# Second attention done tile by tile in pairs of heads, its output columns behind the heads, tile 1's half of it and of the queries placed among the second layer's gathers

## The chip, the core and the metric

The kernel is one program on one core of a Trainium2 chip. The metric is the time of one execution on the device, in microseconds (us). The core has five engines that each run their own list of instructions in order: TensorE (PE in the profile; its weight loads are PEld), VectorE (DVE), ScalarE (ACT), GpSimd (POOL) and SyncE (SP). They wait for each other through semaphores. Matmul results go to four double banks of PSUM, `psA` to `psD`, of 1024 columns each; everything else lives in SBUF, most of it in one array, `arena`, whose parts are used again by later stages. SyncE starts the plain DMAs, GpSimd the indirect ones (gathers) and a few small ones.

## What is computed

One sequence of 256 tokens, 1024 features, all in float32. The first block (multi-scale pooling and a dilated attention, gated and projected) is not touched here. The second block has two layers. Layer 0 is a short convolution mixer, layer 1 is an attention; each is followed by a mixture of very many small experts, called PEER:

```
x = x + conv_mixer(rmsnorm(x))            # layer 0
x = x + peer(rmsnorm(x), layer 0)
x = x + attention(rmsnorm(x)) @ w_o       # layer 1: 16 heads of 64, 4 key/value heads,
x = x + peer(rmsnorm(x), layer 1)         #   window +-128, bias by distance, a sink logit
return rmsnorm(x)

def peer(t):                               # t: 256 tokens x 1024
    q  = (t @ w_q).reshape(256, 8, 2, 128)          # 8 heads, two half queries each
    sc = q . subkeys                                # 8 x 2 x 128 scores for each token
    16 best of each half, their 256 sums, 16 best of these  -> 16 experts for each head
    g  = softmax(of these 16)
    out = sum over 8 x 16 experts of  g * gelu(t . u[e]) * v[e]
```

`u[e]` and `v[e]` lie side by side in memory, so an expert is one row of 8 KB; 16384 experts in each layer. For each token and each of its 128 choices such a row has to be fetched.

## The kernel before, in words

Tokens are two tiles of 128 (one token in each partition). A PEER layer is 16 units (a head and a tile), tile 0's eight first. A unit is 8 groups of 2 experts. A group goes through a ring of 8 places (4 groups): GpSimd gathers 2 x 1 MB (`gathers`, L478), VectorE takes the dot products with `u` (`dots`, L1364), ScalarE makes gelu, coefficient and a diagonal matrix (`mix`, L604 to L614), TensorE adds diagonal times `v` to the tile's sum in PSUM (`weighted`, L966, four products of 512 columns), and then `ring_free` lets GpSimd gather the group four further on. Between its dots VectorE chooses the next unit's experts (L1300 to L1351).

The queries `t @ w_q` come in four chunks of 512 columns. The first chunk's first head is done tile by tile before the gathers (`first_head`), the others for both tiles at once, in slots behind certain groups (`QUERY_SLOTS`): 8 products of 256 columns (L917) in each slot.

Between the layers stands the second attention. After the last group of layer 0, x is added (L1372), normalised (`norm`: a square on ScalarE, then `Sqrt` there with the load of its table, then a chain on VectorE), transposed (L692), keys and values of tile 1 are made (L702, L997). Then a loop runs over two halves of the heads. Each half computes its queries for both tiles (L1019), spreads them into zeroed buffers (L671), and takes 16 units of one head and one tile in a pipeline: scores (L1029, L1030), bias and maximum (L1443, L1444), exponential (L677), transposes (L1036), copy (L1450), product with the values (L1045), division (L1457). After both halves all is transposed, multiplied with the output weights (`mixer`, L711), added and normalised; then first head, choice of experts, and the second layer's gathers begin. All of it lies between the last group of layer 0 and the first gather of layer 1. The program order written in the code sets the order everywhere; SyncE's order of weight loads (`load`, `load_queries`) with its waits sets when weights arrive.

## Time and profile before

| | us |
|---|---|
| runs shown | 2010.59, 2017.71, 2002.35; median 2010.59 |
| the profiled execution, its own time | 2006.81 |
| span from first to last instruction in it | 2005.0 |
| mean TensorE clock granted | 0.968 of full |
| busy: PE, DVE, ACT, POOL | 1672.7, 1060.0, 573.7, 600.9 |
| moved by DMA | 636.14 MB, of it 541.96 on the software queue |

The profile cuts the span in 40 slices of some 50 us. The share of time in which the DMA engines are busy is 9 tenths or more in the slices of the two gather phases and 3, 2 and 0 tenths between them. In the profile's chain that ended last TensorE has 46% and the gathers 26%. Where a group of rows is called by a line, it is a line of the kernel before; some lines are those of helpers (`norm`, `turn`, `turned_out`, `mixer`) and serve several stages.

### The profile page before, as it was taken

Reading aid. Unit: us, or ns where it says so; the run is one execution under the profiler, and the core shown is the slowest. Engines: PE = TensorE matmul, PEld = TensorE weight load, DVE = VectorE, ACT = ScalarE, POOL = GpSimd, SP = SyncE. Lnnn points to the kernel's source line nnn. Section 1 sums busy time; section 2 is a strip of 40 time slices with the busy share of each in tenths; the row PEclk is TensorE's granted clock in tenths of the full one; section 3 lists DMA queues with packets and bytes.
Section 4 is the critical chain, followed back from the end, with each engine's and each line's share of the span. In section 5 each row is a group of like instructions: output and inputs, shape, how many; then the busy total and the mean of one; then the engine's idle time right before and its main releaser. Section 6 shows DMA issues by size and latency. Waiting matters only on the chain.

```text
span 2005.0 us, 18168 instructions
## 1 busy us (share of the span) xinstructions
PE 1672.7 (83%) x5752; PEld 971.0 (48%) x5752; DVE 1060.0 (53%) x2654; ACT 573.7 (29%) x1679; POOL 600.9 (30%) x533
## 2 busy tenths in 40 slices
PE   7999998997989977778877778979989777777776
PEld 5888885975544522223323257665545322223222
DVE  2113102114576657776677424546666776767664
ACT  2111001002333423334333322223343334333332
POOL 1000000001445444444444300023445444444442
PEclk9999999998999989999999989989999999999999
DMA  8544343447899999999999932089999999999996
GB/s 222 136 136 139 126 152 108 160 157 292 349 421 416 421 417 413 421 391 411 413 421 417 399 130 101 0 308 360 421 413 416 421 421 421 391 421 416 421 421 268
DMA packets 147767, 636.14 MB, mean 317 GB/s; under 512 B 9891, under 2 KB 46771, under 8 KB 81884
## 3 DMA queue, kind: packets, MB, share of 16 engines
q0 software_dynamic: 75152, 541.96, 65.9%
q1 hardware_dynamic: 72524, 93.08, 14.1%
q8 instruction: 43, 0.70, 0.1%
q14 instruction: 48, 0.39, 0.0%
HBM read 633.90 MB, written 1.11 MB: 317 GB/s over the span
## 4 chain that ended last, share of the span: by engine, by line
PE 46%; DMA 27%; DVE 12%; issue 7%; ACT 4%; POOL 4%; DVEq 0%; SPq 0%; POOLq 0%; ACTq 0%
DMA arena<-in_peer_uv,arena 26%; PE ps L966 16%; PE ps L723 9%; DVE arena L1364 5%; PE ps L743 4%; POOL arena L478 4%; PE ps L711 4%; PE ps L702 3%; PE ps L917 3%; PE ps L754 2%; PE ps L1019 1%; ACT arena L614 1%; ACT arena L609 1%; PE ps L692 1%; DVE arena L1303 1%
## 5 line engine op out<-in xcount | busy, mean ns | idle before, releaser
L966 PE MATMUL ps<-arena 128*128 128x512 f32 x2048 | 964.3, 618 | 251.5 <-ACT arena L614 251.2
L478 POOL DMA_INDIRECT arena<-in_peer_uv,arena x512 | 587.8, 1148 | 1176.1 <-PE ps L966 563.2
L1364 DVE CUSTOM_DVE_ANT_0 arena<-xn,arena 128x1024 f32<-128x1024 f32 x512 | 622.1, 1225 | 369.2 <-DMA arena<-in_peer_uv,arena 357.8
L966 PEld LDWEIGHTS ps<-arena 128*128 128x128 f32 x2048 | 384.4, 195 | 809.9 <-ACT arena L614 411.4
L604 ACT ACTIVATE arena<-arena 128x2 f32<-128x2 f32 x256 | 52.0, 203 | 783.5 <-DVE arena L1364 779.3
L614 ACT ACTIVATE arena<-const,arena 128x128 f32<-128x128 f32 x512 | 177.6, 394 | 8.3
L723 PE MATMUL ps<-hT,wbuf 128*128 128x256 f32 x704 | 154.7, 382 | 2.6 <-DVE arena L1241 2.6
L723 PEld LDWEIGHTS ps<-hT,wbuf 128*128 128x128 f32 x704 | 134.6, 192 | 21.6 <-DVE arena L1241 3.0
L609 ACT ACTIVATE arena<-arena 128x1 f32<-128x1 f32 x512 | 123.3, 288 | 8.4
L743 PE MATMUL ps<-hT,wbuf 128*128 128x256 f32 x384 | 86.5, 388 | 2.3 <-DMA wbuf<-in_w_in 2.3
L917 PE MATMUL ps<-hT,wbuf 128*128 128x256 f32 x384 | 86.8, 379 | 0.0
L917 PEld LDWEIGHTS ps<-hT,wbuf 128*128 128x128 f32 x384 | 73.0, 190 | 20.2 <-issue 11.5
L743 PEld LDWEIGHTS ps<-hT,wbuf 128*128 128x128 f32 x384 | 74.4, 195 | 14.0 <-issue 3.5
L702 PE MATMUL ps<-hT,wbuf 128*128 128x128 f32 x576 | 72.7, 290 | 8.6 <-DVE x L1137 2.6
L702 PEld LDWEIGHTS ps<-hT,wbuf 128*128 128x128 f32 x576 | 71.4, 206 | 12.5 <-issue 6.0
L1180 DVE COPY arena<-ps 128x384 f32<-128x384 f32 x16 | 8.6, 555 | 108.4 <-PE ps L780 107.5
L711 PE MATMUL ps<-wbuf,arena 128*128 128x512 f32 x128 | 57.3, 608 | 5.2 <-issue 3.8
L493 ACT ACTIVATE xn<-x 128x1024 f32<-128x1024 f32 x14 | 14.7, 1053 | 117.7 <-DVE x L1137 100.8
L1300 DVE MAX8 arena<-arena 128x8 f32<-128x128 f32 (+1 forms) x96 | 29.0, 330 | 33.5 <-ACT arena L651 21.9
L1249 DVE TENSOR_TENSOR arena<-ps,arena 128x1024 f32<-128x1024 f32 x2 | 2.5, 1225 | 81.4 <-PE ps L723 81.4
...
L604 ACT ACT_TABLE_LOAD x34 | 43.6, 1283 | 0.6
(160 smaller groups left out, 1196.3 us busy)
## 6 DMA issues: line engine op xcount, KB each, us to landing
...
wbuf<-in_peer_w_q SPq DMA_DIRECT2D x8, 2048.0 KB, 8.0
wbuf<-in_w_in SPq DMA_DIRECT2D x7, 2048.0 KB, 8.4
wbuf<-in_conv_w_in SPq DMA_DIRECT2D x6, 2048.0 KB, 10.3
arena<-in_peer_uv,arena POOLq DMA_INDIRECT x512
wbuf<-in_attn_w_qkv SPq DMA_DIRECT2D x3, 2048.0 KB, 20.3
wbuf<-in_w_out SPq DMA_DIRECT2D x2, 2048.0 KB
wbuf<-in_conv_w_out SPq DMA_DIRECT2D x2, 2048.0 KB, 7.9
```

The lines of the kernel that those rows point to most:

```text
L478: pool.indirect_dma_start(ring[:, e % RING], None, A["peer_uv"], bass.IndirectOffsetOnAxis(ap=expert[:, unit % 2, e:e + 1], axis=0))\
L604: nc.scalar.activation(act_e[:, b, e0:e0 + GROUP], dot[:, b, e0:e0 + GROUP], ACT.Gelu).then_inc(gelu_done, 1)
L609: last = nc.scalar.activation(coef[:, b, e:e + 1], act_e[:, b, e:e + 1], ACT.Copy, scale=gate[:, b, e:e + 1])
L614: nc.scalar.activation(diag[:, e % RING], ident, ACT.Copy, scale=coef[:, b, e:e + 1]).then_inc(diag_done, 1)
L702: last = mm(dst[:, m * SEQ + t * P:m * SEQ + (t + 1) * P], wbuf[:, b, k, m * P:(m + 1) * P], hT[:, k, t * P:(t + 1) * P], start=(k == 0), ...
L711: last = mm(ps[j][:, t * 512:(t + 1) * 512], src[:, k, t * P:(t + 1) * P], wbuf[:, b, k], start=(k == 0), stop=(k == KC - 1))
L723: last = mm(dst[:, m * SEQ:(m + 1) * SEQ], wbuf[:, b, k, m * P:(m + 1) * P], src[:, k - k0], start=(k == k0), stop=(k == k1 - 1))
L743: last = mm(dst[:, g * SEQ:(g + 1) * SEQ], wbuf[:, b, k, g * P:(g + 1) * P], hT[:, k], start=(k == 0), stop=(k == KC - 1))
L754: last = mm(psB[:, t * 512 + cols_of.start:t * 512 + cols_of.stop], hT4[:, k, t, first:first + P], wbuf[:, 2, k, cols_of], start=(k == 0), ...
L917: last = mm(psC[:, m * SEQ:(m + 1) * SEQ], wbuf[:, b1, k, m * P:(m + 1) * P], hT[:, k], start=(k == 0), stop=(k == KC - 1))
L966: last = mm(ps[t][:, s * 512:(s + 1) * 512], diag[:, e % RING], ring[:, e % RING, D + s * 512:D + (s + 1) * 512], start=False, stop=False, ...
L1364: last = nc.vector.tensor_tensor_reduce(out=ring[:, e % RING, 0:D], in0=xn[:, v // PEER_HEADS], in1=ring[:, e % RING, 0:D], scale=1.0, sca ...
```

## The change

Three things change; the gathers and dot products themselves do not.

**Attention by tile and pairs of heads.** `attend(t)` handles 8 pairs of one tile. A pair's two score products use 64 rows each; VectorE adds bias and takes the maximum in one instruction a head; ScalarE exponentiates in place; VectorE normalises the probabilities before the transposes; ScalarE copies the four transposed blocks; TensorE forms the pair's output already transposed; VectorE copies it into `hT`. For tile 0 the output projection follows pair by pair (`out_step`, two products of 512 columns). The host lays out `w_qkv` and `w_o` by such pairs. The bias comes by two DMAs already in tile form, the sinks lie in a 257th column.

**What stands where.** Tile 0's query and key/value products of the attention move under layer 0's gathers (`KV2_AT`, `Q2_AT`). After the gathers: keys and values of tile 1, `attend(0)`, tile 0's residual and norm, its first head, the gathers of layer 1. Then `attend(1)`; its output projection is in slots behind groups 5 to 12, its residual and norm behind groups 14 and 15 (`OUT_AT`, `RESIDUAL_AT`, `NORM_AT`). PEER's queries go tile by tile in nine parts, slots of 8 products of 128 columns (`PART_SLOTS`); tile 1 of layer 0's mixer is added only behind group 14, too. A fourth weight buffer `w4` is used. In layer 1 the gather of the ring's fourth group waits for all of `attend(1)`'s maxima, since its place held the bias.

**Norm without ScalarE's root.** `norm` on VectorE starts from a guess made of the bits and takes three steps of Newton's method: ten small linked instructions, no table.

```diff
+QUERY_FILLS = (((0, 10), (1, 11), (2, 10)), ((0, 12), (2, 12), (1, 14)))
+FREED_BY = {(0, 10): ("queries", 6), (1, 11): ("queries", 7), (2, 10): ("queries", 8),
+            (0, 11): ("q2", 3), (2, 11): ("q2", 4), (1, 12): ("kv2", 4)}
+KV_FILL, Q_FILLS, OUT_FILL = (1, 12), ((0, 11), (2, 11)), (1, 13)
+MIXER_FILLS = (((0, 7), (1, 7)), ((1, 10), (2, 9)))
+PARTS = ((0, 0), (0, 0), (1, 0), (2, 0), (3, 0), (0, 1), (1, 1), (2, 1), (3, 1))
+NPARTS = len(PARTS)
+PART_SLOTS = {2: (1, 2, 3, 4), 3: (16, 17, 18, 19), 4: (23, 25, 27, 29), 5: (32, 34, 36, 38), 6: (41, 43, 45, 47),
+              7: (50, 52, 54, 56), 8: (60, 62, 64, 66)}
...
+OUT_AT, RESIDUAL_AT, NORM_AT, TURN_AT, TURNED_ACT_AT, TURNED_DVE_AT, CLEAR_AT = 5, 14, 15, 20, 21, 22, 30
+TURN2_AT, TURNED2_AT, KV2_AT, KV2_OUT_AT, Q2_AT, Q2_OUT_AT = 80, 82, 84, 88, (88, 96), (97, 105)
...
+            sp.dma_start(w4, cols(A["peer_w_q_2"][0], 3 * 512, 512)).then_inc(w4_landed, 16)
+            for c, (b, use) in enumerate(QUERY_FILLS[0]):
+                load(b, use, cols(A["peer_w_q_2"][0], c * 512, 512))
...
-            sp.wait_ge(keys_done, ONE + 4)
+            load(*Q_FILLS[0], cols(qkv, 0, 512))
+            load(*KV_FILL, cols(qkv, D, 512))
+            load(*Q_FILLS[1], cols(qkv, 512, 512))
+            sp.wait_ge(keys_done, NPARTS)
...
-            load(0, 12, cols(A["attn_w_o_2"][0], 0, 512))
-            load(1, 13, cols(A["attn_w_o_2"][0], 512, 512))
-            load_queries(1)
+            sp.wait_ge(ring_free, RING_GROUPS + UNITS * UNIT_GROUPS)
+            sp.dma_start(wo2, cols(A["attn_w_o_2"], 512, 512)).then_inc(wo2_landed, 16)
+            load(*OUT_FILL, cols(A["attn_w_o_2"], 0, 512))
+            for c in range(2):
+                load(*QUERY_FILLS[1][c], cols(A["peer_w_q_2"][1], c * 512, 512))
+            sp.wait_ge(av2_done, 16)
+            sp.dma_start(w4, cols(A["attn_w_o_2"], 512, 512)).then_inc(w4_landed, 16)
+            load(*QUERY_FILLS[1][2], cols(A["peer_w_q_2"][1], 2 * 512, 512))
+            sp.wait_ge(out2_done, 1)
+            sp.dma_start(w4, cols(A["peer_w_q_2"][1], 3 * 512, 512)).then_inc(w4_landed, 16)
...
+                if layer == 0:
+                    for b, use in MIXER_FILLS[1]:
+                        pool.wait_ge(chunk_done[b], ONE + use + 1)
+                else:
+                    pool.wait_ge(x_added, 7)
...
+                        if unit == UNITS and g == RING_GROUPS - 1:
+                            pool.wait_ge(max2_done, 2 * HEADS2)
...
+            pool.wait_ge(ring_free, RING_GROUPS + UNITS * UNIT_GROUPS)
+            for t in range(TILES):
+                pool.dma_start(bias2[t][:, :, 0:SEQ], bass.AP(bias_rows2, P * (1 - t), [[1, P], [REL, HEADS2], [1, SEQ]]))\
+                    .then_inc(bias2_loaded[t], 16)
...
-                nc.scalar.activation(root[:, t:t + 1], meansq[:, t:t + 1], ACT.Sqrt).then_inc(root_done, 1)
...
+            def attend(t):
...
+                for p in range(8 + 3):
+                    n = 8 * t + p
+                    if p < 8:
+                        scores_of(n)
+                    if 0 <= p - 1 < 8:
+                        turn_probs(n - 1)
+                    if p - 2 == 0:
+                        pe.wait_ge(v2_copied, 2)
+                    if 0 <= p - 2 < 8:
+                        times_v(n - 2)
+                    if t == 0 and p >= 3:
+                        pe.wait_ge(att2_copied, p - 2)
+                        if p == 3:
+                            pe.wait_ge(w_landed[OUT_FILL[0]], landed_value(*OUT_FILL))
+                            pe.wait_ge(wo2_landed, 16)
+                        out_step(0, 0, p - 3)
+                        last = out_step(0, 1, p - 3)
+                        if p == 10:
+                            last.then_inc(mixer_out, 1)
...
+                for n in range(UNITS * UNIT_GROUPS):
+                    v, g = n // UNIT_GROUPS, n % UNIT_GROUPS
+                    weighted(base + v, v // PEER_HEADS, g)
+                    if n in QUERY_AT and (layer or QUERY_AT[n][0] > 2):
+                        if QUERY_AT[n] == (5, 0):
+                            turned_in((2, 4)[layer], 1)
+                        query_part(layer, *QUERY_AT[n])
...
+                    if layer and OUT_AT <= n < OUT_AT + 8:
+                        j, first = (n - OUT_AT) // 4, (n - OUT_AT) % 4 * 2
+                        if n == OUT_AT:
...
+                        if j:
+                            pe.wait_ge(w4_landed, 32)
+                        out_step(1, j, first)
+                        last = out_step(1, j, first + 1)
+                        if first == 6:
+                            last.then_inc(out2_done if j else chunk_done[OUT_FILL[0]], 1)
...
+            tile_keys(1, 0)
+            tile_keys(1, 1)
+            tile_values(1)
+            pe.wait_ge(edges_zero, 1)
+            pe.wait_ge(q2_copied, 2)
+            pe.wait_ge(k2_copied, 2)
+            attend(0)
...
+            pe.wait_ge(probT2_copied, 8)
+            for j in range(3):
+                tile_queries(psD[:, 0:512], 1, 0, j)
+            pe.wait_ge(x_added, 7)
+            pe.wait_ge(xn_done, step(5, 0))
+            turn(4, 0, xn)
+            tile_queries(psD[:, 0:512], 1, 0, 3)
+            turned_in(4, 0)
+            query_part(1, 0, 0)
+            query_part(1, 0, 1)
+            keys(1, 0)
+            query_part(1, 1, 2)
+            query_part(1, 1, 3)
+            for j in range(4):
+                tile_queries(psD[:, 512:1024], 1, 1, j)
+            keys(1, 1)
+            pe.wait_ge(q2_copied, 4)
+            attend(1)
+            pe.wait_ge(att2_copied, 16)
+            pe.wait_ge(scores_ready, NPARTS + 2)
+            clear(0)
             peer(1)
...
-                link(nc.vector.tensor_scalar(z, z, -0.5, 1.5, ALU.mult, ALU.add))
-                link(nc.vector.tensor_tensor(z, z, y, ALU.mult))
+                link(nc.vector.tensor_scalar(m, sumsq[:, t:t + 1], 1.0 / D, EPS, ALU.mult, ALU.add))
+                link(nc.vector.tensor_scalar(y.bitcast(U32), m.bitcast(U32), 1, None, ALU.logical_shift_right))
+                link(nc.vector.tensor_scalar(y.bitcast(U32), y.bitcast(U32), -1.0, GUESS, ALU.mult, ALU.add))
+                link(nc.vector.tensor_scalar(y, y, NEWTON[0], None, ALU.mult))
+                for n, scaled in enumerate(NEWTON):
+                    to = z if n == len(NEWTON) - 1 else y
+                    link(nc.vector.scalar_tensor_tensor(out=z, in0=y, scalar=m, in1=y, op0=ALU.mult, op1=ALU.mult))
+                    link(nc.vector.scalar_tensor_tensor(out=to, in0=z, scalar=-3.0 * scaled * scaled, in1=y, op0=ALU.add, op1=ALU.mult))
...
+                    if n == RESIDUAL_AT:
+                        residual(1 + layer, 1)
+                    if n == NORM_AT:
+                        norm(3 + 2 * layer, 1, 2 + layer, xn)
...
+                dve.wait_ge(bias2_loaded[t], 16)
+                for p in range(8 + 3):
+                    n = 8 * t + p
+                    if 0 <= p - 3 < 8:
+                        heads_out(n - 3)
+                    if 0 <= p - 1 < 8:
+                        normalise(n - 1)
+                    if p < 8:
+                        row_max(n, 0)
+                        row_max(n, 1)
...
```

Two places of TensorE and one of VectorE show how the instructions move. First TensorE at layer 0's start, from the second half of tile 0's first chunk of queries to the first weighted group, before (L692 transposes normalised x, L702 and L917 are query products, L906 scores, L957 clears the sums, L966 is a weighted group's product):

```order
L702 MATMUL ps<-hT,wbuf 128x128 x16
L692 MATMUL ps<-const,xn 128x128 [waits xn_done,x_added]
L692 MATMUL ps<-const,xn 128x128 x7
L702 MATMUL ps<-hT,wbuf 128x128 [waits tile_turned_dve,tile_turned_act]
L702 MATMUL ps<-hT,wbuf 128x128 x15
...
L702 MATMUL ps<-hT,wbuf 128x128 x16
...
L957 MATMUL ps<-xn,arena 128x512 [waits zeros_ready]
L957 MATMUL ps<-xn,arena 128x512 x3
L966 MATMUL ps<-arena 128x512 [waits diag_done]
L966 MATMUL ps<-arena 128x512
...
L917 MATMUL ps<-hT,wbuf 128x256 [waits pq_copied,w_landed1]
L917 MATMUL ps<-hT,wbuf 128x256 x7
```

Tile 1 is transposed and has its first products ahead of the first weighted group, and eight products of 256 columns stand behind that group. The same place with the change (L968 query products, L985 scores, L992 the clearing, L1089 weighted products):

```order
L968 MATMUL ps<-hT,wbuf 128x128 [waits w_landed0]
L968 MATMUL ps<-hT,wbuf 128x128 x7
L992 MATMUL ps<-xn,arena 128x512 [waits zeros_ready]
L992 MATMUL ps<-xn,arena 128x512
...
L968 MATMUL ps<-hT,wbuf 128x128 [waits pq_copied,w_landed1]
L968 MATMUL ps<-hT,wbuf 128x128 x7
...
L985 MATMUL ps<-arena 128x128 [waits subk_loaded,scores_ready,pq_copied]
L985 MATMUL ps<-arena 128x128 x3
L1089 MATMUL ps<-arena 128x512 [waits diag_done]
L1089 MATMUL ps<-arena 128x512
L1089 MATMUL ps<-arena 128x512 [waits diag_done]
L1089 MATMUL ps<-arena 128x512
```

Tile 1's transposes and products are gone from here; tile 0's second chunk (32 products of 128 columns, of which eight are shown) stands ahead of the first weighted group, and nothing between that group and the next.

Second, TensorE between `attend(0)` and layer 1's gathers with the change (L1024 is the output projection, L1014 the attention's queries of tile 1, L743 transposes):

```order
L1024 MATMUL ps<-wbuf,hT 128x512 [waits att2_copied]
L1024 MATMUL ps<-arena,hT 128x512
L1014 MATMUL ps<-hT,wbuf 128x128 [waits w_landed0,probT2_copied]
...
L743 MATMUL ps<-const,xn 128x128 [waits xn_done,x_added]
L743 MATMUL ps<-const,xn 128x128 x7
L1014 MATMUL ps<-hT,wbuf 128x128 [waits w_landed0]
L1014 MATMUL ps<-hT,wbuf 128x128 x7
L968 MATMUL ps<-hT,wbuf 128x128 [waits w_landed0,pq_copied,tile_turned_dve,tile_turned_act]
L968 MATMUL ps<-hT,wbuf 128x128 x7
L968 MATMUL ps<-hT,wbuf 128x128 [waits w_landed0]
...
L985 MATMUL ps<-arena 128x128 [waits subk_loaded,scores_ready,pq_copied]
```

Layer 1's first query products (L968) wait for weight buffer 0, whose former content the L1014 row just ahead of them reads last.

Third, VectorE where layer 1's experts of the first unit are chosen, with the change (L1465 ends the choice, L1552 takes tile 1's attention queries, L1563 is a maximum of `attend(1)`, L1579 a pair's output, L1471 the gate, L1478 the first dot product):

```order
L1465 TENSOR_TENSOR arena<-arena 128x16 [waits ring_free,dve_step]
L1552 TENSOR_SCALAR arena<-ps 128x4x128 [waits q2_done]
L1563 ISA arena,small<-ps,arena 128x257 [waits probT2_done,sc2_done,bias2_loaded1]
...
L1571 RECIPROCAL small<-small 128x2 [waits exp2_done]
L1573 TENSOR_SCALAR arena<-arena,small 128x256 [waits dve_step]
...
L1571 RECIPROCAL small<-small 128x2 [waits exp2_done]
L1573 TENSOR_SCALAR arena<-arena,small 128x256 [waits dve_step]
L1573 TENSOR_SCALAR arena<-arena,small 128x256
L1579 COPY hT<-ps 128x128 [waits av2_done] x2
...
L1471 RECIPROCAL small<-small 128x1 [waits gate_exp]
L1472 TENSOR_SCALAR arena<-arena,small 128x16 [waits dve_step]
L1478 ISA arena<-xn,arena 128x1024 [waits landed0]
```

The eight pairs of `attend(1)` stand between the choice of experts and the first dot product.

## Rows read from the trace of the kernel before

**Rows 1.** Windows: length, busy us by engine (instructions), TensorE clock, DMA share, GB/s
```profile
1000.00:1150.00 150.00, 113.47 (x240) 44.17 (x238) 97.42 (x225) 49.57 (x161) 64.32 (x58) 0.98 1.01 420
501.50:537.70 36.20, 36.20 (x128) 22.69 (x127) 19.93 (x45) 13.64 (x38) 13.87 (x12) 1.00 0.85 324
1159.00:1173.00 14.00, 6.85 (x39) 6.40 (x39) 4.63 (x13) 3.78 (x8) 3.03 (x2) 0.76 0.63 226
1197.00:1228.00 31.00, 28.75 (x160) 23.28 (x160) 23.76 (x80) 9.05 (x32) 0.00 (x0) 0.87 0.47 172
```
**Rows 2.** Timeline of GpSimd, gathers alone: start, length, engine, line, form, count, idle before
```profile
473.40 1.03 POOL L478 DMA_INDIRECT arena<-in_peer_uv,arena  x1 [279.30 <-DVE arena L1351]
...
501.52 1.65 POOL L478 DMA_INDIRECT arena<-in_peer_uv,arena  x1 [17.64 <-PE ps L966]
...
508.40 1.35 POOL L478 DMA_INDIRECT arena<-in_peer_uv,arena  x1 [3.99 <-PE ps L966]
...
1109.24 0.94 POOL L478 DMA_INDIRECT arena<-in_peer_uv,arena  x1 [2.44 <-PE ps L966]
...
1114.20 0.93 POOL L478 DMA_INDIRECT arena<-in_peer_uv,arena  x1 [2.46 <-PE ps L966]
...
1140.03 0.94 POOL L478 DMA_INDIRECT arena<-in_peer_uv,arena  x1 [2.47 <-PE ps L966]
...
1320.91 0.98 POOL L478 DMA_INDIRECT arena<-in_peer_uv,arena  x1 [157.24 <-DVE arena L1351]
...
1350.16 1.64 POOL L478 DMA_INDIRECT arena<-in_peer_uv,arena  x1 [18.72 <-PE ps L966]
...
1976.63 0.94 POOL L478 DMA_INDIRECT arena<-in_peer_uv,arena  x1 [2.46 <-PE ps L966]
```
**Rows 3.** Timeline of all engines, from the adding of tile 1 on
```profile
1159.12 1.23 DVE L1372 TENSOR_TENSOR x<-ps,x 128x1024 f32<-128x1024 f32 x1 [4.97 <-PE ps L966]
...
1160.38 1.06 ACT L493 ACTIVATE xn<-x 128x1024 f32<-128x1024 f32 x1 [4.76 <-DVE x L1372]
...
1163.34 0.16 DVE L1106 TENSOR_TENSOR rinv<-root 128x1 f32<-128x1 f32 x1
...
1163.53 0.16 DVE L1107 TENSOR_TENSOR rinv<-rinv,meansq 128x1 f32<-128x1 f32 x1
...
1164.92 1.97 PE L692 MATMUL ps<-const,xn 128*128 128x128 f32 x8 [5.84 <-DVE xn L1111]
...
1168.20 5.25 PE L702 MATMUL ps<-hT,wbuf 128*128 128x128 f32 x32 [1.31 <-ACT hT L505]
...
1173.28 3.62 PE L997 MATMUL ps<-wbuf,hT 128*128 128x256 f32 x16
```
**Rows 4.** Groups by line and shape: first attention's row maximum, 384 columns
```profile
L1172 DVE CUSTOM_DVE_ANT_0 ps<-ps,arena 128x384 f32<-128x384 f32 x12 | 6.4, 584 | 0.6 <-PE ps L771 0.6
```
**Rows 5.** The same view, between the layers: exponentials of 257 columns, a copy of 512
```profile
L677 ACT ACTIVATE arena<-ps,small 128x257 f32<-128x257 f32 x32 | 15.3, 477 | 38.4 <-DVE small L1444 38.4
...
L677 ACT ACTIVATION_READ_ACCUMULATOR arena<-ps,small 128x1 f32 x32 | 6.2, 192 | 0.0
...
L502 ACT ACTIVATE hT<-ps 128x512 f32<-128x512 f32 x3 | 1.8, 597 | 9.4 <-PE ps L692 9.4
```
**Rows 6.** Chain of waits, second layer's start: start, length, line, instructions
```profile
1281.72 20.84 PE ps L711 x48
...
1302.56 0.89 PE ps L692 x8
...
1304.27 3.81 PE ps L702 x32
...
1308.59 0.70 PE ps L906 x4
```
**Rows 7.** DMA issues: transfer, queue, count, size, us to landing
```profile
wbuf<-in_peer_w_q SPq DMA_DIRECT2D x8, 2048.0 KB, 8.0
...
arena<-bias_rows POOLq DMA_DIRECT2D x1, 3072.0 KB, 11.8
```

698 lines of the change are left out of this document (354 added, 344 removed).

## The prediction

> **What bounds the kernel now.** I read the windows first, to see which resource is full where. In the middle of a gather phase [rows 1] the DMA queues are full (share 1.01, 420 GB/s) and TensorE is busy for 113.5 of 150 us. Between the phases, in the second attention, the last row has 172 GB/s and TensorE busy for 28.75 of 31 us: no gather runs. Next the gathers by themselves [rows 2]: two rows in the middle (1109.24 and 1114.20) are 4.96 us apart, which is 2 x 1.05 MB at 420 GB/s. 128 groups at this pace are 636 us, and no change that leaves the gathers alone gets below twice that. What can be won is outside: the first layer's gathers start at 473.40, its last group is issued at 1140.03, x is complete at 1159.12 [rows 3], and the second layer starts at 1320.91. So 162 us of chain between the layers gather nothing; the start of each phase loses some more: after four groups the ring is full and the fifth (501.52 and 1350.16) comes 28 and 29 us after the first, because it needs the first weighted group.
>
> I write a phase as: issue of the fifth group, + 123 periods of 4.97 (611 us), + weight loads that share the queues, + a loss, + 19.1 us from the last issue to x (1140.03 to 1159.12). A load of 2 MiB costs 5.0 us at 420 GB/s. In layer 0, 1140.03 - 501.52 = 638.5 us; less 611, less 5.5 MiB of loads issued after the fifth group (by SyncE's list: keys/values, a gain, subkeys, a half of the attention's queries) = 13.7, leaves a loss of 13.8. In layer 1, 1976.63 - 1350.16 = 626.5, no load: a loss of 15.
>
> **Part 1: start of layer 0.** The first gather depends on mixer, norm, first head and choice of experts. The norm is hidden by a mixer product before and still is, so I leave 473.40. From the keys of the first head to the first gather are 11.6 us (in layer 1, where the same stands: 1308.59 + 0.70 to 1320.91) [rows 2, 6]. TensorE after those keys: a mixer part 20.84 / 3 = 6.95, two query products of eight 3.81, clearing two of 512 columns 1.74 (20.84 / 24 is 0.87 each), keys 0.7, the second chunk 7.6, its copy 0.8, keys 1.15: 22.8 us. Scores out, gelu's table and the coefficients take about 3, a weighted group 4 x 0.87 = 3.5, GpSimd 0.8: the fifth group at 30.1 - 11.6 = 18.5 us after the first, 492, against 501.5. The eight first gathers alone take 20 us and a load is still under way, so the queues are full until 498 and I count 2 us more. The query slots of 256 columns go (508.40 - 501.52 = 6.88 us for a group with such a slot; the second row of [rows 1] has 324 GB/s and a full TensorE). In their place stand slots of half the size, and a norm of tile 1 behind group 15, which stops the dot products for square, chain and scaling: 5.8 us from 1159.12 to 1164.92 [rows 3], 4 beyond the slack. One loss against the other: I keep 14. Loads: three halves of the attention's weights, a gain, subkeys = 7.5 MiB, 18.7 us. x complete: 492 + 2 + 611 + 18.7 + 14 + 19.1 = **1157**, only 2 us earlier. Bounds: loss between 6 and 20, so 1149 to 1163.
>
> **Part 2: between the layers**, from x complete (0). Adding x 1.25, square 1.2, ten links of 0.19 (two rows 0.19 apart [rows 3]) in place of table, root and five links, scaling 0.8: 5.2, before 5.8 (1159.12 to 1164.92) [rows 3]. Transposes 1.97, copies 1.3: 8.5. Key products 5.25, values 3.6 as now: 17.3. `attend(0)` waits besides for small instructions of VectorE, the edges and sinks, which lie beside these products. All three loads that must be there fit: the bias in 1 KB pieces, 2 MiB for each tile, against 3 MiB in 11.8 us now [rows 7], the output weights in 8.0 us after 17.3, wanted at about 29. Then `attend(0)`. One pair in a chain: exponentials 0.48 + 0.19 each, a little overlapped, 1.2; normalising, three instructions, an estimate of 0.8 from the 0.8 that scaling 1024 columns takes; transposes 0.45 (0.89 for eight [rows 6]) with 0.25 for hand-overs; the copy 0.6 [rows 5] and 0.1 more: 3.4. The maxima, 0.58 each for 384 columns [rows 4], run beside it. TensorE by pair: scores 0.7 to 0.85, transposes 0.45, values 0.85 to 0.95, output 1.74: 3.8. So 3.4 without, 3.8 with output products. First pair's latency 4.9, two of 3.4, five of 3.8, three output steps and the last value product 6.5: 54.5. No row shows such a pair; 3.0 and 5.3 are my bounds (before, 16 units take some 31 us, two of them 3.9, at clock 0.87 [rows 1]).
>
> Then: adding 1.25, norm 4.6, transposes 1.4, last query product of tile 1 1.8: 63.6. Only now is weight buffer 0 free for layer 1's first chunk, and 8.0 us go by until it is there [rows 7], 0.5 for the issue: 72. TensorE's clock has dropped then: after a wait of 5.84 the eight transposes took 1.97, against 0.89 behind mixers, and two heads' products 5.25 against 3.81 [rows 3, 6]; the granted clock of that stretch is 0.76 [rows 1], part of it at 1.2 GHz, the rest at 2.4. I take 4.9 for the first two products. From their end to the first gather are 12.8 (1304.27 + 3.81 to 1320.91). The first gather is at **90** us (82 to 102) in place of 162: 72 us won. A wait is new here, the 8 us for the chunk; behind it on TensorE stand all of tile 1's queries and `attend(1)`.
>
> The Trainium skill, "DMA: Bandwidth & Descriptors", section on the anatomy of a DMA, has 2.0 us plus bytes at 436 GB/s. By it the load would be 6.8 us and the sum 1.2 us less; the trace's 8.0 is the measured one and I use it.
>
> **Part 3: start of layer 1.** The order of VectorE puts `attend(1)` between choice and dots. Three groups of gathers are issued, the fourth after the last maximum (28 us), so the ring fills but is not used. Latency 4.9 and seven pairs of 3.4, values and copy 1.4, gate 0.5, two dots 2.5, ScalarE 1.2, weighted 3.5, GpSimd 0.8: 38.6; I take 40 (35 to 55) to the fifth group, now 29. So tile 1's attention is hidden by the first 20 us of gathers and shows for 11 us. Behind it, groups 1 to 12 have slots of 1.7 to 1.8 us: 5.2 us on TensorE, hardly over 4.97. Loads after the fifth group: two query chunks and a gain, 4.5 MiB, 11.2. Loss 14 as in part 1. x complete: 40 + 611 + 11.2 + 14 + 19.1 = 695 after the first gather, now 674.8.
>
> **Sum**: 1157 + 90 + 695 = 1942, end 8.7 later (9.3 before, less the table): span 1951, and 1.8 us around it (2006.81 - 2005.0): **1953 us**, against 2006.8, which lies 0.2% under the median of 2010.6. That is 2.9% less. Own range of this case 1935 to 1972.
>
> **Rivals.**
> 1. *Quicker at every start* (0.15): pairs at 3.0 (10 us), loss 8 in each layer (12 us): 1931. For it: half the slots' columns. Against: the norm behind group 15.
> 2. *Pairs slow* (0.2): 5.3 us for a pair, if the hand-overs on three engines do not overlap and TensorE runs at half clock in the thin stretch. 16 x 1.7 = 27: 1980. For it: before, a unit is dense (28.75 of 31 us) and yet at clock 0.87. The Trainium skill, "TensorE: Matmul & The Clock Gate", section on the transposes, says that transposes do not count as activity for the clock, and that inactivity leaves it at half rate. By that, the two products after the wait and much of `attend(1)` would be slow; the rows at 1164.92 agree as to the wait, and no row here shows a thin attention.
> 3. *The hidden half comes back* (0.07): fifth group of layer 1 at 80 instead of 40, if weights, `attend(1)` and queries queue behind the chunk's wait, as well as 5 us more in layer 0. About 1998, within 1%.
> 4. *Slower* (0.03): pairs go one after another. A pair alone is scores 0.7, maxima 1.2, chain 3.4, values 0.95, copy 0.3, hand-overs 0.5: 7; with TensorE's 2.7 doubled, 9.7. 16 x 6.1 = 97: 2050. It decides from 8.6 us a pair on (77 us over the forecast, 2030). Against it: waits in the order only reach back one to three pairs.
> 5. That the change does not do what it says: the order shows the products where they are said to be, but `attend(1)` is beside gathers only, not beside dots; this is in the sum.
>
> **Numbers.** Forecast 0.55, rivals 0.15, 0.2, 0.07, 0.03. Range 1928 to 1985: it takes in rivals 1 and 2 and leaves out some 0.15. 1% is 20 us, about what a measurement of this kernel can tell from none. Faster by more 0.91, within 0.06, slower 0.03.
>
> **What would show it.** Fifth group of layer 0 at about 492 and last x near 1157; first gather of layer 1 about 90 us after it; TensorE idle for some 7 us ahead of layer 1's first query products; 3.4 to 3.8 us from pair to pair; fifth group of layer 1 some 40 us after the first. Wrong if pairs pass 5 us, or a group in the steady part takes more than 5.0 us.

## The result and the profile after

The changed kernel takes **1953.65 us** in the median of 4 runs (1950.94 to 1958.15), the kernel before 2008.3 (4 runs beside it): the ratio is 0.973, 95% interval 0.968 to 0.977. The profiled execution took 1950.94 us, its span is 1949.1. The forecast was 1953, with a span of 1951.

First the gathers of the changed kernel, GpSimd's timeline (columns as in [rows 2]): first and fifth group of layer 0 and its last issue, then first, fourth and fifth group of layer 1 and the last issue.

```profile
474.07 1.03 POOL L522 DMA_INDIRECT arena<-in_peer_uv,arena  x1 [279.24 <-issue]
...
498.32 0.94 POOL L522 DMA_INDIRECT arena<-in_peer_uv,arena  x1 [14.09 <-PE ps L1089]
...
1136.55 0.94 POOL L522 DMA_INDIRECT arena<-in_peer_uv,arena  x1 [2.46 <-PE ps L1089]
...
1247.79 1.00 POOL L522 DMA_INDIRECT arena<-in_peer_uv,arena  x1 [89.47 <-DVE arena L1465]
...
1273.80 0.94 POOL L522 DMA_INDIRECT arena<-in_peer_uv,arena  x1 [18.64 <-issue]
...
1288.62 0.94 POOL L522 DMA_INDIRECT arena<-in_peer_uv,arena  x1 [12.59 <-PE ps L1089]
...
1921.11 0.94 POOL L522 DMA_INDIRECT arena<-in_peer_uv,arena  x1 [2.47 <-PE ps L1089]
```

Against [rows 2]: layer 0 keeps its start and ends 3.5 us sooner; the first gather of layer 1 has moved from 1320.91 to 1247.79, and the fifth group now comes 40.8 us after it where it came 29.3 after before. The fourth stands apart from the third: it goes to places that tile 1's bias held until the last maximum of `attend(1)`.

Next what stands between x complete and that first gather, the timeline of all engines (some rows out of many), and last the row at which x of layer 1 is complete:

```profile
1155.63 1.22 DVE L1486 TENSOR_TENSOR x<-ps,x 128x1024 f32<-128x1024 f32 x1 [4.97 <-PE ps L1089]
...
1160.98 1.97 PE L743 MATMUL ps<-const,xn 128*128 128x128 f32 x8 [5.38 <-DVE xn L1235]
...
1170.00 3.62 PE L1006 MATMUL ps<-wbuf,hT 128*128 128x256 f32 x16
...
1212.02 1.22 DVE L1262 TENSOR_TENSOR x<-ps,x 128x1024 f32<-128x1024 f32 x1 [3.32 <-PE ps L1024]
...
1220.87 0.37 SPq L424 DMA_DIRECT2D wbuf<-in_peer_w_q  x1
...
1229.04 5.95 PE L968 MATMUL ps<-hT,wbuf 128*128 128x128 f32 x32 [8.20 <-DMA wbuf<-in_peer_w_q]
...
1236.01 3.74 PE L968 MATMUL ps<-hT,wbuf 128*128 128x128 f32 x32
...
1940.19 1.23 DVE L1486 TENSOR_TENSOR x<-ps,x 128x1024 f32<-128x1024 f32 x1 [4.97 <-PE ps L1089]
```

x is complete at 1155.63, so the gap to the gather is 92.2 us (161.8 before). `attend(0)` with its output products fills 1173.6 to 1212. Then comes the new wait: weight buffer 0 is free at 1220.87, the chunk is there 8.2 us later, and the two products behind it take 5.95 us; the same 32 instructions take 3.74 directly after. The pairs of heads, TensorE's timeline, two in `attend(0)` (scores L1035, transposes L1044, values L1055, output L1024) and four transposes of `attend(1)`, with the rows between the first two:

```profile
1193.33 0.70 PE L1035 MATMUL ps<-arena 64*128 64x256 f32 x4
...
1193.97 0.66 PE L1044 MATMUL ps<-const,arena 128*128 128x128 f32 x4
...
1194.55 0.66 PE L1055 MATMUL ps<-arena 128*64 128x128 f32 x8
...
1195.15 1.13 PE L1024 MATMUL ps<-wbuf,hT 128*128 128x512 f32 x2
...
1196.11 1.02 PE L1024 MATMUL ps<-arena,hT 128*128 128x512 f32 x2
...
1197.06 0.70 PE L1035 MATMUL ps<-arena 64*128 64x256 f32 x4
...
1258.30 1.11 PE L1044 MATMUL ps<-const,arena 128*128 128x128 f32 x4 [0.30 <-DVE arena L1573]
...
1259.34 1.13 PE L1055 MATMUL ps<-arena 128*64 128x128 f32 x8
...
1260.40 1.23 PE L1035 MATMUL ps<-arena 64*128 64x256 f32 x4
...
1261.93 1.12 PE L1044 MATMUL ps<-const,arena 128*128 128x128 f32 x4 [0.30 <-DVE arena L1573]
...
1269.20 0.66 PE L1044 MATMUL ps<-const,arena 128*128 128x128 f32 x4 [0.83 <-DVE arena L1573]
...
1272.38 0.66 PE L1044 MATMUL ps<-const,arena 128*128 128x128 f32 x4 [1.29 <-DVE arena L1573]
```

In `attend(0)` one row follows the other without idle time and the period is 1197.06 - 1193.33 = 3.73 us: TensorE sets it. In `attend(1)` the same transposes take 1.11 instead of 0.66 us, and the period is 3.63 although the output products are gone. Only its last pairs are quick again: 0.66 us, and 1272.38 - 1269.20 = 3.18 from one to the next, with TensorE idle for 1.29 us ahead of the transposes instead of 0.30. The windows (columns as in [rows 1]) say why:

```profile
1180.00:1189.00 9.00, 8.16 (x32) 4.57 (x32) 4.00 (x18) 3.15 (x10) 0.00 (x0) 0.50 0.09 30
1189.00:1212.00 23.00, 22.99 (x116) 11.03 (x115) 8.00 (x34) 6.89 (x21) 0.00 (x0) 1.00 0.00 1
1229.00:1236.00 7.00, 6.49 (x36) 6.33 (x37) 0.00 (x0) 0.38 (x1) 0.00 (x0) 0.68 0.00 0
1247.00:1268.00 21.00, 16.17 (x84) 9.65 (x82) 9.86 (x44) 9.35 (x31) 5.85 (x6) 0.59 0.96 379
1290.00:1340.00 50.00, 50.00 (x171) 26.56 (x170) 34.67 (x88) 17.95 (x56) 19.79 (x19) 1.00 0.98 380
```

The granted clock is 1.00 in the dense part of `attend(0)`, 0.50 (all of it at 1.2 GHz) just before and 0.59 in `attend(1)`. The last row is the start of layer 1's steady part: TensorE busy all 50 us, DMA share 0.98.

| us | before | after | difference |
|---|---|---|---|
| start to x complete, layer 0 | 1159.1 | 1155.6 | -3.5 |
| x complete to the first gather of layer 1 | 161.8 | 92.2 | -69.6 |
| from there to x complete, layer 1 | 674.8 | 692.4 | +17.6 |
| end | 9.3 | 8.9 | -0.4 |
| span | 2005.0 | 1949.1 | -55.9 |

The experiments take apart only some of the 69.6 us. None undoes the pairs of heads as such, or puts tile 0's query, key and value products back between the layers, so how much each of these two gives stays open.

### The profile page after: what moved, and what is told of

Read it like the earlier page. It is cut to its first block, busy times and chain, and to the rows that moved or that the text cites. A ratio compares the mean times of both kernels' runs of the same rounds, so it can differ in the third digit from the quotient of the medians.

```text
span 1949.1 us, 18676 instructions
## 1 busy us (share of the span) xinstructions
PE 1655.1 (85%) x6184; PEld 966.1 (50%) x6184; DVE 1049.2 (54%) x2676; ACT 554.3 (28%) x1664; POOL 587.3 (30%) x533
## 3 DMA queue, kind: packets, MB, share of 16 engines
HBM read 637.05 MB, written 1.11 MB: 327 GB/s over the span
## 4 chain that ended last, share of the span: by engine, by line
PE 45%; DMA 31%; DVE 9%; issue 6%; ACT 4%; POOL 3%; another core or an unknown queue 0%; SPq 0%; DVEq 0%; POOLq 0%; ACTq 0%
DMA arena<-in_peer_uv,arena 30%; PE ps L1089 17%; PE ps L774 9%; DVE arena L1478 5%; PE ps L794 4%; POOL arena L522 3%; PE ps L762 3%; PE ps L805 2%; PE ps L968 2%; PE ps L753 1%; PE ps L1024 1%; ACT arena L664 1%; ACT arena L659 1%; PE ps L1044 1%; ACT arena L654 1%
## 5 line engine op out<-in xcount | busy, mean ns | idle before, releaser
L1089 PE MATMUL ps<-arena 128*128 128x512 f32 x2048 | 966.6, 617 | 221.3 <-ACT arena L664 220.6
L522 POOL DMA_INDIRECT arena<-in_peer_uv,arena x512 | 574.7, 1123 | 1134.9 <-PE ps L1089 597.6
L1478 DVE CUSTOM_DVE_ANT_0 arena<-xn,arena 128x1024 f32<-128x1024 f32 x512 | 622.4, 1225 | 374.9 <-DMA arena<-in_peer_uv,arena 358.6
L1089 PEld LDWEIGHTS ps<-arena 128*128 128x128 f32 x2048 | 380.7, 195 | 752.1 <-issue 391.7
L774 PE MATMUL ps<-hT,wbuf 128*128 128x256 f32 x704 | 154.7, 382 | 2.6 <-DVE arena L1360 2.6
L774 PEld LDWEIGHTS ps<-hT,wbuf 128*128 128x128 f32 x704 | 134.6, 192 | 21.6 <-DVE arena L1360 3.0
L968 PEld LDWEIGHTS ps<-hT,wbuf 128*128 128x128 f32 x768 | 94.0, 196 | 27.1 <-issue 26.1
L968 PE MATMUL ps<-hT,wbuf 128*128 128x128 f32 x768 | 94.7, 279 | 9.0 <-DMA wbuf<-in_peer_w_q 8.2
L794 PE MATMUL ps<-hT,wbuf 128*128 128x256 f32 x384 | 86.7, 388 | 3.0 <-DMA wbuf<-in_w_in 3.0
L794 PEld LDWEIGHTS ps<-hT,wbuf 128*128 128x128 f32 x384 | 74.5, 195 | 14.7 <-issue 4.2
L805 PE MATMUL ps<-wbuf,arena 128*128 128x256 f32 (+1 forms) x256 | 43.0, 329 | 0.0
L762 PEld LDWEIGHTS ps<-wbuf,arena 128*128 128x128 f32 x128 | 24.7, 195 | 36.3 <-issue 34.5
L1478 DVE DVE_READ_ACCUMULATOR2_ANT arena<- 128x1 f32 x512 | 42.2, 82 | 0.0
```

Of the source, the lines that this page charges most:

```text
L522: pool.indirect_dma_start(ring[:, e % RING], None, A["peer_uv"], bass.IndirectOffsetOnAxis(ap=expert[:, unit % 2, e:e + 1], axis=0))\
L762: last = mm(ps[t][:, j * 512:(j + 1) * 512], src[:, k, t * P:(t + 1) * P], wbuf[:, b, k], start=(k == 0), stop=(k == KC - 1))
L774: last = mm(dst[:, m * SEQ:(m + 1) * SEQ], wbuf[:, b, k, m * P:(m + 1) * P], src[:, k - k0], start=(k == k0), stop=(k == k1 - 1))
L794: last = mm(dst[:, g * SEQ:(g + 1) * SEQ], wbuf[:, b, k, g * P:(g + 1) * P], hT[:, k], start=(k == 0), stop=(k == KC - 1))
L805: last = mm(psB[:, t * 512 + cols_of.start:t * 512 + cols_of.stop], hT4[:, k, t, first:first + P], wbuf[:, 2, k, cols_of], start=(k == 0), ...
L968: last = mm(products[:, m - first], w[:, k, m * P:(m + 1) * P], hT[:, k, t * P:(t + 1) * P], start=(k == 0), stop=(k == KC - 1))
```

## The experiments

Each is timed in 5 rounds against the kernel before, in three sets, each on a chip of its own (e0 to e3, e4 to e7, e8 to e10; e8's expectation says call for set). "x to 1st" is from x complete to the first gather of layer 1 in the run's trace, "to 5th" from there to the fifth group.

| run | median us | ratio, 95% | x to 1st | to 5th |
|---|---|---|---|---|
| e0 changed kernel again | 1952.9 | 0.9713, 0.9679 to 0.9746 | 91.5 | 40.5 |
| e1 norm only | 2016.95 | 1.0003, 0.9973 to 1.0033 | 174.6 | 29.0 |
| e2 chunk early | 1944.58 | 0.9672, 0.9639 to 0.9706 | 84.8 | 39.8 |
| e3 output after the heads | 1962.8 | 0.9764, 0.9729 to 0.9798 | 102.8 | 40.9 |
| e4 first gathers late | 1956.32 | 0.9743, 0.9725 to 0.9762 | 115.6 | 19.4 |
| e5 products of zeros | 1944.39 | 0.968, 0.9661 to 0.9699 | 90.3 | 37.9 |
| e6 chunk early, 2 | 1938.38 | 0.9643, 0.9623 to 0.9662 | 83.3 | 39.8 |
| e7 attention in one piece | 1959.29 | 0.9755, 0.9736 to 0.9774 | 123.9 | 18.3 |
| e8 changed kernel again | 1950.78 | 0.9703, 0.9669 to 0.9737 | 90.8 | 40.5 |
| e9 before, with zeros | 2002.79 | 0.9966, 0.9946 to 0.9987 | 159.3 | 29.1 |
| e10 e6 with zeros | 1937.72 | 0.9633, 0.96 to 0.9666 | 82.7 | 37.5 |

In the changed kernel's variants the second set is some 3 us quicker in one place of layer 0, told at the end (x complete at 1152.1 to 1152.8, in the other two at 1153.4 to 1159.2), and has no run of the changed kernel itself. So kernels of different sets are compared by the intervals of their traces. One trace gives an interval with a scatter of its own: the 123 groups behind layer 1's fifth took 631.8 to 635.9 us in the three traces of the changed kernel.

**e0 and e8: the change as it is.**

> The changed kernel once more, for an interval beside the others on the same chip: 1950 to 1957 us, ratio to the kernel before 0.970 to 0.975.

> The changed kernel on the chip of the two next runs. In the second call layer 0's fifth group came 3 to 5 us earlier in all four kernels than in the first call's, since ScalarE's copy of the third part's queries waited 5.05 us there and 8.53 us here. So 1948 to 1953 us, with the fifth group at 493 to 498.

Both came out as expected.

**e1: the norm alone.** Before's kernel with this in its norm, and no square root on ScalarE:

```diff
-                act.wait_ge(meansq_done, step(k, t))
-                nc.scalar.activation(root[:, t:t + 1], meansq[:, t:t + 1], ACT.Sqrt).then_inc(root_done, 1)
+                link(nc.vector.tensor_scalar(y.bitcast(U32), m.bitcast(U32), 1, None, ALU.logical_shift_right))
...
```

> The kernel before, with the changed kernel's norm alone (Newton steps on VectorE, no square root on ScalarE). Theory (the gain is the chain between the layers): a norm that is exposed gets 0.45 us shorter (5.80 to 5.35 us from x to the transposes), and the tables that ScalarE reloads around nine square roots go, of which at most the ones between and behind the layers are waited for. 1 to 5 us less than before, from x complete to the first gather of layer 1 still 160 us, ratio 0.9975 to 0.9995. Rival (the norm carries a large part of the gain, since the square root and its two table loads of 1.28 us stand in front of gelu and coefficients): 10 us less or more, ratio 0.995 or below.

The ratio says no difference, and the 12 runs fall in two groups: 5 at 2001.9 to 2006.7, 7 at 2016.7 to 2022.3. Before's own 17 runs do so too: 12 at 2004.7 to 2010.6, 5 at 2017.6 to 2027.7. Lower group against lower group (medians 2005.8 and 2007.2) the norm is worth between 1 and 2 us, which 5 runs can't tell from nothing, and no more than 5.4 by the interval. It does not carry the gain. Its trace happened to be of the upper group, with 174.6 us between x and the first gather against 161.8 in the trace of before, and shows what makes it. TensorE's timeline in the second attention's second half (L1030 is the scores of one unit):

```profile
1283.27 1.20 PE L1030 MATMUL ps<-arena 128*128 x2
...
1285.83 1.20 PE L1030 MATMUL ps<-arena 128*128 x2
```

Two windows, the first from that half's query products on into its units, the second the units alone:

```profile
1232.00:1272.00 40.00, 35.35 (x142) 30.55 (x141) 12.34 (x38) 9.41 (x27) 0.00 (x0) 0.71 0.15 52
1272.00:1296.00 24.00, 23.12 (x97) 20.74 (x96) 13.38 (x45) 4.85 (x16) 0.00 (x0) 0.51 0.00 0
```

A unit each 2.56 us, at a clock of 0.51; in the kernel before such rows are 1.65 us apart once the clock is up:

```profile
1207.55 0.68 PE L1030 MATMUL ps<-arena 128*128 x2
...
1209.20 0.68 PE L1030 MATMUL ps<-arena 128*128 x2
```

The window of the kernel before that corresponds to the first of the two has 0.90:

```profile
1228.00:1262.00 34.00, 28.80 (x142) 24.40 (x143) 11.11 (x35) 8.83 (x25) 0.00 (x0) 0.90 0.18 62
```

So the attention before had two speeds, and the times of the kernel before fall in both groups with one and the same program. That asked for e9.

**e9: the kernel before, with its idle time in the attention filled.** TensorE waits 4.64 us there, twice, for ScalarE's copies of the queries. TensorE's timeline before, the second of the two (L1019 is the queries, L1029 the first unit's sinks):

```profile
1228.29 14.08 PE L1019 MATMUL ps<-hT,wbuf 128*128 128x256 f32 x64 [0.56 <-DVE arena L1457]
...
1247.01 0.58 PE L1029 MATMUL ps<-sinks,const 128*128 x2 [4.64 <-ACT arena L671]
```

The edit puts five products of zeros into each wait:

```diff
                 last.then_inc(chunk_done[2], 1)
+                for _ in range(5):
+                    mm(psB[:, 0:512], zeros, xn[:, 0, 0:512], start=True, stop=True)
                 pe.wait_ge(q2_copied, c + 1)
```

> The kernel before with five products of zeros of 512 columns (4.3 us) in the second attention behind each half of the queries, where TensorE waits 4.64 us for ScalarE's copies. Theory (the times before fall in two groups, 2002 to 2011 and 2016 to 2028, because units of that attention come each 2.56 us at half the clock and 1.65 us at the full one, and whether the clock recovers is chance): the wait no longer lets the clock fall, all runs come out between 1998 and 2008, none above 2012, median 4 to 8 us under before's. Rival (the two groups come from gathers or the chip): a third of the runs still above 2015.

All 12 runs lie between 2000.3 and 2009.3, eleven of them below 2004.1; 4 of the 17 runs of before beside them were above 2015. The window that corresponds now has the full clock:

```profile
1226.00:1262.00 36.00, 34.52 (x179) 26.95 (x179) 14.83 (x48) 10.54 (x31) 0.00 (x0) 1.00 0.16 58
```

The ratio, 0.9966, is clear of noise, and the runs lie some 4 us under before's lower group (median 2006.6 in this set); 2.5 us of it are in the gap. None of the 12 is in the upper group; with 10 of 43 runs there before, that alone could be chance, at something between 1 in 10 and 1 in 25. Together with the clock of 0.51 in e1's slow trace and of 1.00 here it says that the two groups come from TensorE's clock in the attention. The change gains by group: 54 us against the lower (2007.2 to 1952.9), 66 against the upper (2019.0).

**e3: the output products of tile 0 in one block** behind the last pair, which undoes one part of the change:

```diff
-                        out_step(0, 0, p - 3)
-                        last = out_step(0, 1, p - 3)
                         if p == 10:
+                            for c in range(KC):
+                                out_step(0, 0, c)
+                                last = out_step(0, 1, c)
                             last.then_inc(mixer_out, 1)
```

> The changed kernel with the sixteen output products of tile 0 in one block after the last pair instead of one pair behind. Theory (the products fill idle time of TensorE between the hand-overs of a pair): pairs then come each 3.2 to 3.6 us as in attend(1) instead of 3.73, the last values end at about 52 us after x, and the block costs 8 x 1.91 = 15.3 us behind it, more where the clock is down: the first gather of layer 1 comes 11 to 16 us later than 92.2, 1962 to 1970 us, ratio 0.977 to 0.981. Rival (TensorE sets the pairs and only the sum of its work counts): 0 to 3 us later, 1951 to 1957.

9.9 us more than e0, with 11.3 more in the gap: the low end of what was expected. The pairs did not get quicker without the output products. TensorE's timeline, transposes of two pairs:

```profile
1191.61 1.11 PE L1044 MATMUL ps<-const,arena 128*128 128x128 f32 x4 [0.30 <-DVE arena L1574]
...
1195.24 1.11 PE L1044 MATMUL ps<-const,arena 128*128 128x128 f32 x4 [0.30 <-DVE arena L1574]
```

The windows over the pairs and over the block behind them:

```profile
1186.00:1215.00 29.00, 25.00 (x113) 14.14 (x110) 10.48 (x46) 9.54 (x31) 0.00 (x0) 0.52 0.00 1
1215.00:1228.00 13.00, 13.00 (x46) 6.89 (x45) 1.22 (x1) 0.68 (x1) 0.00 (x0) 1.00 0.01 1
```

3.63 us a pair at a clock of 0.52, and 1.00 as soon as the block of output products runs. So with its output products a pair takes only 0.1 us more than without them at half clock (0.55 more than without them at full clock, by e5), and the block of some 13 us is gone from the chain.

**e5: is it the clock?** The changed kernel, with eight products of zeros in the wait for the chunk and one in each pair of `attend(1)`:

```diff
+            def filler(n, dst, cols=512):
+                for _ in range(n):
+                    mm(dst[:, 0:cols], zeros, xn[:, 0, 0:cols], start=True, stop=True, skip_group_check=True)
...
                     if p < 8:
                         scores_of(n)
+                        if t == 1:
+                            filler(1, psA)
...
             turned_in(4, 0)
+            filler(8, psD[:, 512:1024])
             query_part(1, 0, 0)
```

> The changed kernel with products of zeros whose results nobody reads: eight of 512 columns while TensorE waits for the chunk, and one in each pair of attend(1). Theory (TensorE ran at half its clock there only because it had been idle): the two products behind the wait take 3.7 us instead of 5.95, transposes and values of attend(1) 0.66 each instead of 1.12, its pairs come each 3.2 us instead of 3.63: 4 to 5 us less in all, 1947 to 1950 us, ratio 0.969 to 0.971. Rival (the pairs' time is hand-overs between the engines, and the filler only queues before the transposes): attend(1) as long as now or longer, 1952 or more.

TensorE's timeline, the two products behind the wait, then transposes of two pairs of `attend(1)`:

```profile
1226.20 3.84 PE L968 MATMUL ps<-hT,wbuf 128*128 128x128 f32 x32 [1.16 <-DMA wbuf<-in_peer_w_q]
...
1255.64 0.66 PE L1049 MATMUL ps<-const,arena 128*128 128x128 f32 x4 [0.24 <-DVE arena L1581]
...
1258.82 0.66 PE L1049 MATMUL ps<-const,arena 128*128 128x128 f32 x4 [0.24 <-DVE arena L1581]
```

The window over the pairs:

```profile
1247.00:1268.00 21.00, 17.37 (x108) 8.35 (x104) 11.09 (x51) 10.80 (x35) 3.60 (x5) 1.00 0.83 340
```

3.84 us instead of 5.95, transposes 0.66 instead of 1.11, 3.18 us from pair to pair instead of 3.63, clock 1.00: in every row as the theory said. The work is the same and more, at twice the clock. The last pairs of the changed kernel, above, say the same without any product of zeros (0.66 us, 3.18 apart), and so do those of e7 (3.17). From x complete to the fifth group it is 128.1 us against 131.2 to 133 in the three traces of the changed kernel. The total, 1944.4, is 3 us lower than the range, as much as the sets differ. The gain in the total is not shown as firmly as the one in the rows: from x to x the trace has 783.8 us, against 784.6, 787.0 and 782.1 in the changed kernel's, since its 123 groups behind the fifth took 636.6. At half clock a pair loses only 0.45 us, though its three rows are together 1.45 us longer (3.47 against 2.02): the rest falls into time in which TensorE is idle at full clock. The Trainium skill, "TensorE: Matmul & The Clock Gate", part on the PE-mode transpose, says that transposes don't count as busy for the clock. The traces neither show nor refute it: in e3 TensorE is busy in 25 of 29 us, a third of it transposes, and the clock stays down, but in the last pairs of `attend(1)` and from the sixth pair's scores on in e7's it rises in the midst of the same transposes. No run here had the same pairs without them.

**e2 and e6: the new wait.** The chunk of layer 1 can be loaded early if the queries that hold its buffer are done early. Four of tile 1's query products go into the first two pairs of `attend(0)`, the other four under the norm:

```diff
                     if p < 8:
                         scores_of(n)
+                    if t == 0 and p == 0:
+                        for j in range(3):
+                            tile_queries(psD[:, 512:1024], 1, 0, j)
                     if 0 <= p - 1 < 8:
                         turn_probs(n - 1)
+                    if t == 0 and p == 1:
+                        tile_queries(psD[:, 512:1024], 1, 0, 3)
...
-                tile_queries(psD[:, 0:512], 1, 0, j)
+                tile_queries(psD[:, 0:512], 1, 1, j)
...
-            for j in range(4):
-                tile_queries(psD[:, 512:1024], 1, 1, j)
```

> The changed kernel with tile 1's first four query products of the attention inside the first two pairs of attend(0) (psD's second half, copied out before values use it), and the other four under the norm, so that weight buffer 0 is free at about 25 us after x and the chunk of layer 1 is long there. Theory (the 8.2 us wait for the chunk and the cold products behind it are on the chain): the first gather of layer 1 comes 81 us after x complete instead of 92.2 (transposes and copies done at 64, two products at full clock 3.8, then 12.8), the fifth group still 41 later; 10 to 12 us less than the changed kernel, 1941 to 1945 us, ratio to before 0.966 to 0.968. Rival (another transfer or VectorE's chain of choices is behind the wait, or the four products delay the first pairs by their 3.6 us and the gain is spent): 3 us or less, 1948 or more.

> The version of e2 with the copy of the four early products behind the maxima of the second pair instead of before them. Theory (in e2 VectorE waited 5.6 us for the fourth product with the second pair's maxima behind it, which made attend(0) 3 us longer than the changed kernel's): x to the first gather 81 to 82 us, 2 to 4 us less than e2: 1941 to 1943 us, ratio 0.965 to 0.967. Rival (the early products themselves cost TensorE the 3 us): as e2, 1944 or more.

e2 gave 8.3 us (against e0), less than expected. VectorE's timeline shows the loss: the copy of the four products waits 5.56 us, and the maxima of the second pair (L1568) stand behind it.

```profile
1183.72 0.69 DVE L1557 TENSOR_SCALAR arena<-ps 128x512 f32<-128x512 f32 x1 [5.56 <-PE ps L1014]
...
1184.33 0.41 DVE L1568 CUSTOM_DVE_ANT_0 arena<-ps,arena 128x257 f32<-128x257 f32 x1
```

e6 has the copy behind those maxima:

```diff
-                    if t == 0 and p == 1:
-                        queries2_out(1, 0, psD)
                     if p < 8:
                         row_max(n, 0)
                         row_max(n, 1)
+                    if t == 0 and p == 1:
+                        queries2_out(1, 0, psD)
```

Its timeline, where the wait was:

```profile
1216.27 1.06 PE L743 MATMUL ps<-const,xn 128*128 128x128 f32 x8 [0.65 <-DVE xn L1243]
...
1218.96 3.74 PE L968 MATMUL ps<-hT,wbuf 128*128 128x128 f32 x32
...
1235.49 1.00 POOL L522 DMA_INDIRECT arena<-in_peer_uv,arena  x1 [80.61 <-DVE arena L1470]
```

The two products follow the transposes and the attention's last query products without a wait, at full clock, and the gap is 83.3 us: 1.5 less than e2 where 3 were expected, since `attend(0)` still ends 2 to 3 us later than without the early products. The total is 6.2 us under e2's and below the range given, but half of that is the difference between the sets. x to the fifth group: 123.0 us, 8 to 10 less than in the changed kernel. So the wait and the half clock behind it, new in this change, cost some 8 to 10 us.

**e4 and e7: what the gathers beside tile 1's attention are worth.** In e4 they merely start later, in e7 (built on e6) both attentions stand before the norm:

```diff
-                    pool.wait_ge(x_added, 7)
+                    pool.wait_ge(max2_done, 2 * HEADS2)
```
```diff
+            pe.wait_ge(q2_copied, 4)
+            attend(1)
             pe.wait_ge(x_added, 7)
             pe.wait_ge(xn_done, step(5, 0))
             turn(4, 0, xn)
...
+            queries2_out(1, 1, psD)
+            attend(1)
-            peer(1, attend)
+            peer(1)
```

> The changed kernel, where GpSimd starts layer 1's gathers only after the last maximum of attend(1), so that no gather runs beside tile 1's attention; the rest is in its old order. Theory (a phase counts from its fifth group, which waits for VectorE's dots behind attend(1), and the ring holds three or four groups in any case): first gather at about 118 us after x complete in place of 92, the first four groups land in 20 us from there, fifth group issued 0 to 5 us later than now: 1952 to 1958 us, ratio 0.972 to 0.975. Rival (a phase moves with its first gather, so that the 26 us of gathers beside the attention are what is won there): 20 us more or over, 1973 or above, ratio 0.983 or above.

> The version of e6 with attend(1) directly behind attend(0) on all engines, ahead of tile 0's addition, norm and first head: the attention of both tiles stands before the first gather. Theory: 31 to 33 us more before the first gather (about 114 us after x), but the fifth group then comes about 20 us after it instead of 40: 10 to 15 us more than e6, 1951 to 1957 us, ratio 0.971 to 0.974. Rival (the order under the gathers hides the whole half of the attention): 28 us or more over e6, 1970 or above.

e4: the first gather comes 24 us later, the fifth group 2 to 4, and x of layer 1 is complete 791.2 us after x of layer 0, against 784.6, 787.0 and 782.1 in the changed kernel's traces. 4 to 9 us, of which the fifth group explains 2 to 4 and the rest lies in the groups behind it, whose time scatters by as much: a little more than expected, and a small part of the 24. The fifth group is the better mark. e7 is 20.9 us behind e6, in the traces 17.4: more than the 10 to 15 expected, less than the rival's 28. GpSimd's and VectorE's timeline (adding tile 0, first gather, fifth group):

```profile
1249.01 1.21 DVE L1266 TENSOR_TENSOR x<-ps,x 128x1024 f32<-128x1024 f32 x1
...
1275.98 1.00 POOL L522 DMA_INDIRECT arena<-in_peer_uv,arena  x1 [121.18 <-DVE arena L1469]
...
1294.32 0.94 POOL L522 DMA_INDIRECT arena<-in_peer_uv,arena  x1 [8.41 <-PE ps L1096]
```

`attend(1)` with its queries costs 38.8 us in the gap (tile 0's addition stands 96.9 us after x, 58.1 in e6), of which the earlier fifth group (18.3 after the first instead of 39.8) gives 21.5 back. So placing it beside the first gathers hides about half of it.

**e10: both together.** e6 with the products of zeros of e5 in `attend(1)`, and four around the third part's keys in layer 0:

```diff
+                        if t == 1:
+                            filler(1 if p else 8, psA)
...
+            filler(1, psD)
             keys(0, 2)
+            filler(3, psD)
             peer(0)
```

> The version of e6 with products of zeros in attend(1) (eight behind the first pair's scores, one in each further pair) and four around the third part's keys in layer 0. Theory: pairs of attend(1) 3.2 us apart instead of 3.63, so the fifth group of layer 1 comes 36 to 37 us after the first instead of 39.8; the first weighted group of layer 0 takes 3.7 us instead of up to 6: 13 to 17 us less than the changed kernel beside it, 1932 to 1937 us. Rival (products of zeros delay what follows them as much as the clock gives back): as e6, 10 to 11 us less than the changed kernel.

13.1 us under e8, the low end, and with 1937.7 just above the range. Pairs are 3.17 us apart; the fifth group of layer 1 comes at 37.5, a little later than 36 to 37. In layer 0 it comes 4.4 us after the start of the first weighted group, in e8 6.6, at a clock of 0.50; but the products of zeros also hold that group back, and of the 2.1 us 1.0 is left from the first gather to the fifth group. It is the fastest of this case, ratio 0.9633. What the products of zeros add to the early chunk no two runs of one set show. e6 has 0.9643 in the quicker set; from x to the fifth group e10 has 120.2 us against e6's 123.0, from x to x 774.6 against 775.4, which is less than the scatter.

## Why the prediction was right, step by step

The gain is where it was put, the chain between the layers. Of its terms:

- **Start of layer 0.** First gather 474.07 (473.40). Fifth group 498.3 where 492 was worked out, 494 with the 2 us added: too early by 4. Two terms were too small. The first weighted group ran at half clock (0.50 in its first 4 us), some 6 us instead of 3.5; so it did in every variant without products of zeros there. And ScalarE's copy before it waited 3.5 us longer (last section); where that copy did not (e4 to e7) the fifth group came at 493 to 495.
- **Loss** in layer 0: 1136.55 - 498.32 - 611 - 18.7 = 8.5, not 14; in layer 1: 1921.11 - 1288.62 - 611 - 11.2 = 10.3 (before 626.5 - 611 = 15.5, not 15). I had set the smaller query slots and the norm of tile 1 against each other in full; the norm costs one group of 10 us in place of 5 (the twentieth, in both layers), and the slots, by this reckoning alone and not tried by themselves, gave some 10. One trace does not size it either: e0 and e8, the same kernel, have losses of 8.5 and 9.9 in layer 0, 13.7 and 9.6 in layer 1, so the 14 holds in one of six. Rival 1's "quicker at every start" was half right here: most losses nearer to its 8 than to 14, pairs not.
- **x complete** 1155.6 for 1157: two errors that cancel.
- **Between the layers** 92.2 for 90. Norm to transposes 5.35 for 5.2 (three of the ten links start 0.25 us apart, not 0.19). Keys and values end at 18.0 for 17.3. Pairs with output 3.73 for 3.8, and TensorE sets them, as said. End of `attend(0)` 56.4 for 54.5: the first pairs ran at half clock, which the sum did not have. The wait for the chunk 8.2 for 8.5, foreseen with its place. The prediction quotes 6.8 beside its 8.0. The Trainium skill, "DMA: Bandwidth & Descriptors", section on the anatomy of a DMA, gives that fit for DMAs that GpSimd issues; this load is SyncE's, and it took 8.2. The two products behind it 5.95 for 4.9: more of it at half clock than taken (window 1229 to 1236: 0.68; at full clock 3.74). The last 12.8 exact.
- **Start of layer 1.** Fifth group 40.8 after the first for 40. The pairs of `attend(1)` at 3.63 for most of it instead of 3.4 because of the clock; at full clock they are 3.18 (its own last ones, and e5).
- **Rival 2**, slow pairs: the clock did fall in the thin attention, as it said, but a pair lost 0.45 us by it, where the rival had 1.7, as at full clock TensorE has idle time in a pair (1.29 us, at half clock 0.30). **Rival 3**: no more than 0.8 of its 40 us came back. **Rival 4**: pairs overlapped.
- The errors sum to -2 us: span 1949.1 for 1951. That is luck in part, since single terms were off by 4 to 6.
- Left out: that the kernel before had two speeds. The profile it was forecast from was of the lower group; against the upper one the gain is 12 us more.
